# Seven half products instead of eight for the u and r weights of the first block

## The reference, cut to what matters

```
h_lat, h_ctx = modulate(rmsnorm(x)), modulate(rmsnorm(ctx))     # 1024 and 256 tokens
u, v, q, k, vv, r, af, ab, ga, gb = split(h @ w_in)             # u, v, vv, r, ga, gb: 1024 columns each
lf, lb = log_sigmoid(af @ w_af + b_af) / 16, ...                # the decays
o = scan over chunks of 64 tokens with q, k, vv, lf, lb         # both directions
b_lat = norm(o) * silu(r);  a_lat = gelu(u) * mixed(layernorm(gelu(v)))
y = sigmoid(ga) * (a_lat @ w_a) + sigmoid(gb) * (b_lat @ w_b)
```

## Time and profile before

| | |
|---|---|
| median of 3 runs | 3249.92 us (3249.72 to 3252.65) |
| the profiled execution's own time | 3249.49 us |
| its span, first to last instruction | 3248.2 us |
| PE busy | 3175.4 us, 98% of the span |
| DVE, ACT, POOL busy | 1892.3, 1408.1, 393.3 us |
| granted PE clock | 0.993 of full |

### The profile page before, as it was taken

The page is one execution under the profiler, slowest core; times in us unless marked ns, Lnnn a source line. Parts: engine busy times, 40 slices in busy tenths (PEclk is TensorE's granted clock), DMA queues, the critical chain, the costliest instruction groups (busy, mean ns, idle before and its releaser), DMA issues.

```text
span 3248.2 us, 38749 instructions
## 1 busy us (share of the span) xinstructions
PE 3175.4 (98%) x14558; PEld 2584.2 (80%) x14558; DVE 1892.3 (58%) x3053; ACT 1408.1 (43%) x2336; POOL 393.3 (12%) x625
## 2 busy tenths in 40 slices
PE   6999999999999999999999999999899999999998
PEld 4888788888888878888888887877667888888886
DVE  5562344565334487777444546656686787776443
ACT  4791232254333243333233376575576443333221
POOL 1111000012000200000010200112221200001011
PEclk8999999999999999999999999999999999999999
DMA  5564544456542323334763444355876432336652
GB/s 231 180 223 157 166 149 155 127 209 217 177 143 101 132 98 111 112 115 144 242 197 95 144 136 137 124 172 170 178 114 154 149 123 104 123 104 216 207 189 68
DMA packets 228489, 495.13 MB, mean 152 GB/s; under 512 B 21712, under 2 KB 84816, under 8 KB 226768
## 3 DMA queue, kind: packets, MB, share of 16 engines
q1 hardware_dynamic: 146688, 298.11, 29.2%
q0 software_dynamic: 81616, 194.55, 19.0%
HBM read 353.63 MB, written 138.94 MB: 152 GB/s over the span
## 4 chain that ended last, share of the span: by engine, by line
PE 85%; DVE 7%; ACT 3%; DMA 2%; issue 2%; POOL 0%; SPq 0%; DVEq 0%; POOLq 0%; ACTq 0%
PE p L2273 12%; PE p L2275 12%; PE p L2274 12%; PE p L319 12%; PE p L321 11%; PE p L320 11%; PE p L420 2%; PE p L421 2%; PE p L422 2%; PE p L3341 1%; PE p L1287 1%; PE p L3327 1%; PE p L1276 1%; DMA s_qs<-d_q2l 1%; DMA s_ad<-i_ada 1%
## 5 line engine op out<-in xcount | busy, mean ns | idle before, releaser
L319 PE MATMUL p<-s_xh,s_wh 128*128 128x512 f32 x1936 | 767.1, 396 | 9.8 <-DVE s_tmp L476 6.0
L321 PE MATMUL p<-s_xh,s_wl 128*128 128x512 f32 x1936 | 754.9, 390 | 0.0
L320 PE MATMUL p<-s_xl,s_wh 128*128 128x512 f32 x1936 | 754.3, 390 | 0.0
L2273 PE MATMUL p<-s_xh,s_wh 128*128 128x512 f32 x1152 | 449.7, 390 | 1.5 <-DVE s_wl L2522 1.3
L2275 PE MATMUL p<-s_xh,s_wl 128*128 128x512 f32 x1152 | 448.3, 389 | 0.0
L2274 PE MATMUL p<-s_xl,s_wh 128*128 128x512 f32 x1152 | 448.2, 389 | 0.0
L319 PEld LDWEIGHTS p<-s_xh,s_wh 128*128 128x128 f32 x1936 | 363.6, 188 | 96.6 <-issue 11.1
L321 PEld LDWEIGHTS p<-s_xh,s_wl 128*128 128x128 f32 x1936 | 363.5, 188 | 76.8
L320 PEld LDWEIGHTS p<-s_xl,s_wh 128*128 128x128 f32 x1936 | 363.8, 188 | 74.3 <-issue 1.9
L278 DVE TENSOR_TENSOR s_wl<-s_ws,s_wh 128x1024 fp32r<-128x1024 f32 x143 | 176.7, 1247 | 208.6 <-ACT s_wh L271 208.3
L464 ACT ACTIVATE s_tmp<-p 128x512 f32<-128x512 f32 (+1 forms) x157 | 93.0, 593 | 429.3 <-PE p L321 340.8
(11 more groups left out here) (437 smaller groups left out, 5497.4 us busy)
## 6 DMA issues: line engine op xcount, KB each, us to landing
d_h<-s_fhl POOLq DMA_DIRECT2D x80, 512.0 KB, 3.0
s_ws<-i_Wf SPq DMA_DIRECT2D x48, 512.0 KB, 4.2
s_qb<-i_Wf SPq DMA_DIRECT2D x40, 512.0 KB, 4.2
s_qb<-i_Wf SPq DMA_DIRECT2D x80, 256.0 KB, 2.9
s_ws<-i_Wf SPq DMA_DIRECT2D x80, 256.0 KB, 2.8
s_aw<-i_adaT SPq DMA_DIRECT2D x32, 512.0 KB, 3.7
s_xh<-d_h POOLq DMA_DIRECT2D x16, 1024.0 KB, 12.3
s_xl<-d_h POOLq DMA_DIRECT2D x16, 1024.0 KB, 15.4
```

What stands on the lines that cost most here:

```text
L319: pe.matmul(o, wh, H[:, k, c:c + n], start=(k == 0), stop=False)
L320: pe.matmul(o, wh, L[:, k, c:c + n], start=False, stop=False)
L321: last = pe.matmul(o, wl, H[:, k, c:c + n], start=False, stop=(k == 7))
L2273: pe.matmul(o, wh[:, c], H[:, k, :], start=(start and k == 0), stop=False)
```

## The change

The order of weights becomes ga 0 to 2, v, ga 3 to 7, gb; u and r leave the list of fill jobs.

- **Pairs.** u and r are made at the end of stage 1, as 8 pairs of two weight tiles (256 output rows). A pair is a product of two by two blocks: four blocks of weights (128 outputs by 512 inputs) with four of tokens (512 inputs by 512 tokens). It is made from seven units, each 4 k tiles by 3 matmuls, 12 matmuls of 512 columns. Partial results are passed from bank to bank by ACT (`seeded`), P5 is held in SBUF (`held`) and added by DVE when P7 and P3 are taken out. Two matmuls mark banks 5 and 6 as written before the first pair.
- **Sums.** DVE makes the four combined token blocks once (40 operations of 128x512, 16 low parts, ACT 16 high parts), beside stage 1's jobs 21 to 26, and for each pair four combined weight blocks (`fold_dve`). High and low parts of units are made by halves of a tile, seven units ahead.
- **Pieces.** In the last job of the second vv group and of both v groups, the four weight tiles of the group are taken one after the other, so that each frees its place early: 96 matmuls of 128 columns in place of 24 of 512.
- **Places.** Raw tiles of v and vv use `ACC` and `RB` too, and only the first vv group uses the second set of places.
- **Moved.** Stage 1 has 31 fill jobs, with the decay units two at a time behind chosen jobs (Abs twice, Exp twice, Ln twice) and 8 of the dots; the other 24 dots run beside the pairs, three in each, behind P5, P2 and P4. Stage 2 has 22 fill jobs: ga 0 to 2 (6) and both v groups (16), three in slot 0 and one in each slot after it. Stage 3 has 26, and the norms, mixes and outputs of its second half move one job up and on.

The diff, cut to its core:

```diff
-    for n in ("v", "u", "r", "ga", "gb"):
-        order += [(n, m) for m in range(8)]
+    order += [("ga", m) for m in range(3)] + [("v", m) for m in range(8)]
+    order += [("ga", m) for m in range(3, 8)] + [("gb", m) for m in range(8)]
...
+SEVEN = ("P1", "P5", "P6", "P2", "P7", "P3", "P4")
+SEVEN_TILES = [(n, m) for n in ("u", "r") for m in range(0, 8, 2)]
+SEVEN_FIRST = 17
...
+        x = 2 + m % 2 if name in ("v", "vv") and m % 4 > 1 else i if i < NW else i % NS
...
+            p.pieces = []
+            if chunk == chunks[-1][0]:
+                p.pieces = pieces
+                for a in pieces[:-1]:
+                    used[i - 3 + a] = mm.at(more("mm"))
...
+        for a in p.pieces:
+            for k in range(8):
+                xh, xl = H[:, k, p.col:p.col + 128], L[:, k, p.col:p.col + 128]
+                wh, wl = WHg[:, a, k * 128:k * 128 + 128], WLg[:, a, k * 128:k * 128 + 128]
+                pe.matmul(o[:, a, :], xh, wh, start=(k == 0), stop=False)
+                pe.matmul(o[:, a, :], xl, wh, start=False, stop=False)
+                last = pe.matmul(o[:, a, :], xh, wl, start=False, stop=(k == 7))
+            last.then_inc(*mm.up())
+        if p.pieces:
+            return
...
-            plan_rows(jobs, "vv", group, banks, dV, "v", of_context + token_chunks(2, (0, 1)))
-        plan_rows(jobs, "v", 0, banks, dVm, "vm", token_chunks(0, (0, 1)))
+        plan_rows(jobs, "vv", 0, banks, dV, "v", of_context + token_chunks(2, (0, 1)))
+        second_places_done = jobs[-1].mm
+        plan_rows(jobs, "vv", 1, banks, dV, "v", of_context + token_chunks(2, (0, 1)), (1, 2, 3, 0))
+        context_done = jobs[22].mm
...
+        decay_after = (0, 1, 3, 4, 6, 8, 9, 11, 12, 14, 16, 17, 19)
+        dot_after = (2, 5, 7, 10, 13, 15, 18, 20)
+        steps = []
+        for j in range(31):
+            steps += [("before", j), ("fill", j)]
+            if j in dot_after:
+                steps.append(("dot", dot_after.index(j)))
+            if j in decay_after:
+                steps.append(("decay", decay_after.index(j)))
...
+        def difference_dve(o, one, other):
+            (h1, l1), (h2, l2) = one, other
+            dv.tensor_tensor(o, h1, h2, ALU.subtract).then_inc(*summed.up())
+            DVW.wait_ge(*summed.now())
+            dv.tensor_tensor(o, o, l1, ALU.add).then_inc(*summed.up())
+            DVW.wait_ge(*summed.now())
+            dv.tensor_tensor(o, o, l2, ALU.subtract).then_inc(*summed.up())
...
+            dv.tensor_tensor(THL[t][1][:, k, :], TF[t][:, k, :], THL[t][0][:, k, :].bitcast(F), ALU.subtract).then_inc(*t_lo.up())
...
+        B11, B21, B22 = ((XH[:, k:k + 4, c:c + 512], XL[:, k:k + 4, c:c + 512]) for k, c in ((0, 0), (4, 0), (4, 512)))
+        INPUT = {"P1": B11, "P2": B21, "P3": B22, "P5": THL[1], "P6": THL[2], "P7": THL[3], "P4": THL[4]}
+        BANK = {"P1": BA, "P5": BF, "P6": BB, "P2": BA, "P7": BE, "P3": BB, "P4": BE}
...
+                u.slot = (2 + u.i) % 8
+                u.hi, u.lo, u.mm = u_hi.at(u.i + 1), u_lo.at(u.i + 1), mm.at(more("mm"))
+                u.slot_free = units[u.i - 8].mm if u.i >= 8 else used[13 + u.slot // 2]
...
+        dots_of_pair = [range(8 + 24 * n // n_pairs, 8 + 24 * (n + 1) // n_pairs) for n in range(n_pairs)]
...
+            for i in range(2):
+                sp.dma_start(x[:, 1024 * i:1024 * i + 1024], D["W" + p.name][p.m + i]).then_inc(*raw[2 * (p.n % 2) + i].up())
...
+            for p in pairs:
+                if p.n + 2 < n_pairs:
+                    load_pair_sp(pairs[p.n + 2])
+                elif p.n + 2 == n_pairs:
+                    weights_sp(SEVEN_FIRST + NS)
+                for j in dots_of_pair[p.n]:
+                    if j + 1 < 32:
+                        dot_sp(j + 1)
+            weights_sp(SEVEN_FIRST + NW + NS)
...
+        def unit_pe(u, fresh):
+            wh, wl = half_tile(u.slot)
+            o = B[u.bank][:, :]
+            PEW.wait_ge(*u.hi)
+            PEW.wait_ge(*u.lo)
+            H, L = u.x
+            for k in range(4):
+                c = slice(128 * k, 128 * k + 128)
+                for t in u.x_ready[k]:
+                    PEW.wait_ge(*t)
+                pe.matmul(o, wh[:, c], H[:, k, :], start=(fresh and k == 0), stop=False, skip_group_check=not fresh)
+                pe.matmul(o, wh[:, c], L[:, k, :], start=False, stop=False, skip_group_check=not fresh)
+                x = pe.matmul(o, wl[:, c], H[:, k, :], start=False, stop=(k == 3), skip_group_check=not fresh)
+            x.then_inc(*mm.up())
...
+            for b in (BB, BE):
+                for t in first_free[b]:
+                    PEW.wait_ge(*t)
+                pe.matmul(B[b][:, :], XH[:, 0, 0:128], XH[:, 0, 0:512], start=True, stop=True)
+            for p in pairs:
+                for name in SEVEN:
+                    if name == "P1":
+                        for t in ([pairs[p.n - 1].outs["P2"].ev] if p.n else first_free[BA]):
+                            PEW.wait_ge(*t)
+                    elif name == "P5":
+                        for t in ([pairs[p.n - 1].held] if p.n else first_free[BF]):
+                            PEW.wait_ge(*t)
+                    elif name in ("P6", "P2"):
+                        PEW.wait_ge(*p.seed1)
+                    elif name in ("P7", "P3"):
+                        PEW.wait_ge(*p.seed2)
+                    elif name == "P4":
+                        PEW.wait_ge(*p.outs["P7"].ev)
+                    unit_pe(p.units[name], name in ("P1", "P5"))
...
+            ac.activation(half_tile(u.slot)[0], u.src, ACT.Copy).then_inc(*u_hi.up())
...
+        def pair_act(p, name):
+            u = p.units[name]
+            if name == "P1":
+                ACW.wait_ge(*u.mm)
+                for t in ([pairs[p.n - 1].outs["P3"].ev] if p.n else first_free[BB]):
+                    ACW.wait_ge(*t)
+                ac.activation(B[BB][:, :], B[BA][:, :], ACT.Copy).then_inc(*seeded.up())
+            elif name == "P5":
+                ACW.wait_ge(*u.mm)
+                if p.n:
+                    ACW.wait_ge(*pairs[p.n - 1].outs["P3"].ev)
+                ac.activation(HELD[:, :], B[BF][:, :], ACT.Copy).then_inc(*held.up())
+            elif name == "P6":
+                ACW.wait_ge(*u.mm)
+                for t in ([pairs[p.n - 1].outs["P4"].ev] if p.n else first_free[BE]):
+                    ACW.wait_ge(*t)
+                ac.activation(B[BE][:, :], B[BB][:, :], ACT.Copy).then_inc(*seeded.up())
+            elif name in ("P2", "P4"):
+                out_act(p.outs[name], u.bank, u.mm)
...
+            high_act(6)
+            for u in units:
+                pair_act(pairs[u.n], u.name)
+                high_act(u.i + 7)
+                tail_weights(weights_act, u)
...
+            if units[i].name == "P5":
+                DVW.wait_ge(*p.raw0)
+                DVW.wait_ge(*p.raw1)
+                DVW.wait_ge(*(pairs[p.n - 1].units["P3"].lo if p.n else w_lo.at(SEVEN_FIRST)))
+                dv.tensor_tensor(S1, p.A21, p.A22, ALU.add).then_inc(*folded.up())
+                DVW.wait_ge(*p.s[0])
+                dv.tensor_tensor(S2, S1, p.A11, ALU.subtract).then_inc(*folded.up())
+            elif units[i].name == "P7":
+                if p.n:
+                    DVW.wait_ge(*pairs[p.n - 1].units["P7"].lo)
+                dv.tensor_tensor(S3, p.A11, p.A21, ALU.subtract).then_inc(*folded.up())
+            else:
+                DVW.wait_ge(*p.s[1])
+                dv.tensor_tensor(S4, p.A12, S2, ALU.subtract).then_inc(*folded.up())
...
+                dv.tensor_tensor(l, u.src, h.bitcast(F), ALU.subtract).then_inc(*u_lo.up())
...
+            dv.tensor_tensor(TMP[:, o.slot, :], B[u.bank][:, :], HELD[:, :], ALU.add).then_inc(*evD.up())
...
+            for i in range(7):
+                low_dve(i)
+            for u in units:
+                p = pairs[u.n]
+                pair_dve(p, u.name)
+                fold_dve(u.i + 8)
+                low_dve(u.i + 7)
+                for j, after in zip(dots_of_pair[p.n], ("P5", "P2", "P4")):
+                    if u.name == after:
+                        mod_dve(j)
+                tail_weights(weights_dve, u)
+            mods_end_dve()
...
-        items = [("u", m, False, "plain", dU, "u", 1.0, TC) for m in range(8)] + [("r", m, False, "plain", dR, "r", 1.0, TC) for m in range(8)]
+        items = [("ga", m, False, "plain", dGA, "ga", 1.0, TC) for m in range(3)]
         banks = [0, 1]
-        jobs = []
-        plan_rows(jobs, "v", 1, banks, dVm, "vm", token_chunks(0, (0, 1)))
-        for j in range(4):
-            jobs[2 * j].make = 26 + j
-        rows_done = jobs[7].mm
-        jobs += plan_fill(items, banks, None, parts, [])
+        jobs = plan_fill(items, banks, None, parts, [])
+        plan_rows(jobs, "v", 0, banks, dVm, "vm", token_chunks(0, (0, 1)), (0, 1, 2, 3))
+        plan_rows(jobs, "v", 1, banks, dVm, "vm", token_chunks(0, (0, 1)), (0, 1, 2, 3))
+        for p in jobs:
```

(92 more changed lines are left out.)

277 lines of the change are left out of this document (211 added, 66 removed).

## The result

The changed kernel takes 3264.17 us (3262.23 to 3269.65, 5 runs), the kernel before 3249.92 (3248.23 to 3252.65, 5 runs): ratio 1.0047, interval 1.0036 to 1.0058. It is slower by 14 us. The forecast was 3240.0 us (3225 to 3256), so it missed by 24.2 us and in sign. The profiled execution took 3262.23 us.

What follows compares the result with a forecast made beforehand. PE, busy 98% of the span, was taken as the bound. Terms -21.8 + 0.5 + 15.3 - 5.2 + 1.0 + 0.2 + 0.3 = -9.7 us took 3249.5 to 3239.8, stated as 3240 us, range 3225 to 3256.

Steps and rivals of the forecast that it cites:

- What lies beside other work: Stage 1 and pairs: ACT's and DVE's work stays covered by PE's; only +0.3 us, for eight pairs of products.
- the signs of being wrong that the prediction names: The pieces' step is off, or PE gains long waits in the pairs or in stage 2's slots.
- Products, -21.8: u and r, end of stage 1: 672 matmuls of 512 columns instead of 768, 96 fewer at 0.2276 us, -21.8 us.
- the rival of the dots: Pairs of products: dots bound them if adaT landings slow to 5.5 us (3252) or 6 us (3264); 13%.
- Pieces, +15.3: Three row jobs: 96 matmuls of 128 columns for 24 of 512, 0.110 us each, +5.1 us a job, +15.3 us.
- both rivals of its size: Pieces: weight loads hide (0.057 us, 3224.5 to 3231.5, 12%), or float32 pace (0.248 us, 3279.5, 10%).
- Start of stage 2, -5.2: Stage 2's start: 5.5 us lost to idle time and fallen clock; three jobs cover it, 0.3 us stays: -5.2 us.
- Slots of stage 2 and stage 3: Stage 2: one job covers each slot, about 12.8 us in the later half, +1.0 us; stage 3: jobs moved, +0.2 us.
- the +1.0 of the forecast: Stage 2's slots: the state product's wait for ACT's key copy, 0.7 us each time, grows by 1.05.

Runs made afterwards that it cites:

- e1: Kernel before with only stage 1's decay units two at a time, at the changed kernel's places among the jobs: 3265.87 us, ratio 1.0053.
- e2: Changed kernel with the second half of each decay pair (subtraction and scans) right behind its first half in VectorE's order: 3252.39 us, ratio 1.0012.
- e8: Changed kernel with the edit of e2, and stage 1's eight dots moved behind job 20: 3245.12 us, ratio 0.9992.
- e10: Changed kernel with the decay units using four banks in turn instead of two: 3262.13 us, ratio 1.0045.
- e5: Changed kernel with its 24 decay units one at a time, spread over the same 20 jobs, dots unmoved: 3256.15 us, ratio 1.0023.
- e4: Changed kernel with the three row jobs of stages 1 and 2 whole again, without pieces: 3257.19 us, ratio 1.0027.
- e6: Kernel of e2 with stage 2's first job ahead of the first slot's gate step in every engine's order: 3247.89 us, ratio 1.0001.
- e7: Kernel of e6 with the three row jobs whole again, without pieces: 3240.47 us, ratio 0.9971.

## Why the prediction was wrong

**The step that failed** stands under "What lies beside other work": "ACT in stage 1 loads its tables half as often; before, it was 64% busy there and PE never waited." It costed the decay pairs at nothing from a busy share and a count of loads. The share was an average over 227 us; from 95 to 225 us, where the decay units run, ScalarE was busy 88% (113.91 of 130). The table loads did fall, from 42 to 22 in that stretch, and ScalarE's busy time to 84.36 us. But a share of busy time says nothing of a loop with only two buffers: one unit at a time left the other buffer for the next Abs; two at a time leave none. In short, what ScalarE saved in loads it lost in waiting for scans (34.9 us). And the loop, 10.6 us a pair, had only 8.8 us of PE's work to hide behind, since the units also moved closer together. No rival held this mechanism, and the signs of being wrong that the prediction names, waits in the pairs of products or in the slots, look elsewhere. Shown by e1 (+17 us by the pairs at this spacing, with no new products), e2 and e8 (back by the order of scans and dots, pairs and spacing kept), e10 (not PE's banks). The missing term is +18.7 us. What grouping and spacing each cost alone was not run in the kernel before.
The Trainium skill (ScalarE: Activation LUTs, Rules for kernel authors) advises to do all of one table set before switching. Here doing so about halved the loads, and e1, which does it, is 17 us slower. With the scans no longer behind other work, the pairs (e2, 3252.39) ran 3.8 us under single units in the same jobs (e5, 3256.15).

**Products, -21.8**: right. The pairs run from 300.3 to 452.68 us, 152.4 us, where 153 were expected, without a wait. Outputs of P7 cost nothing that shows, and the rival of the dots falls: the 23 rows of `adaT` from 300 to 455 us landed in a median of 3.7 us, as before.

**Pieces, +15.3**: the step of 0.111 us was taken as 0.110, so both rivals of its size are out. The 0.110 was the middle between two rows and not derived, so its fit is partly luck. The Trainium skill (TensorE: Matmul & The Clock Gate, Back-to-back issue gap) gives about 81 ns for a sustained pair at 128 columns; these float32r matmuls took 0.111 us. Three jobs cost 15.6 us of PE. What the term left out is the other side, the stalls that whole jobs would have: net, the pieces cost 7.0 us (e4) and 7.4 (e6 to e7). The change is better without them; as a term beside the kernel before, +15.3 stands.

**Start of stage 2, -5.2**: right in kind, too large. "The third job needs job 0's bank, which ACT copies behind its first exponentials, at about the same time" saw the queue and priced it at 0.3 us. From 452.68 to the first transposes are 18.8 us, against some 16.7 foreseen: +2.1, with PE idle 2.17 and the granted clock at 1.00. In e2 the same wait was 3.33, and moving one line of the order brought 4.5 us.

**Slots of stage 2 and stage 3**: right. A slot takes 679.43 - 666.64 = 12.79 us, as foreseen, and PE is idle in none of the later ones. The slowest key copy makes PE wait 1.68 us instead of 0.74, and the four waits for it sum to 3.9 us against 2.9: the +1.0 of the forecast. In stage 3 PE is idle 0.9 us, as before.

**The account.** Stage 1 +18.7 and stage 2's start +2.1 make 20.8 of the miss of 24.2. At 1.1 ms both kernels run the same code; a line of it in the kernel after, then in the one before:
```profile
1114.65 0.95 PE L2003 MATMUL p<-s_ones,s_acc 128*128 128x1 f32 x8
```
```profile
1103.08 0.94 PE L1648 MATMUL p<-s_ones,s_acc 128*128 128x1 f32 x8
```
+11.6 there, where -9.7 was forecast: a miss of 21.3. Of the last 3 us, 1.1 arise behind this place, in code that didn't change (2146.2 us to the end of the span against 2145.1); PE's waits at L332 for VectorE are 7.4 us against 6.0 there. The other 1.9 are no part of this trace: the profiled execution of the changed kernel took 3262.23 us, 1.9 under the median. No run tells more, and both are within what executions of one kernel differ by.

## What to carry to other kernels

Before grouping units to save a fixed cost on one engine, write down the loop through the buffers they share: what must end before the next group may begin, on every engine, with what is queued ahead of it. If the group takes all buffers, the engines take turns, and the loop's length has to be less than the work it hides behind; busy shares don't show it, least of all averaged over a stage in which the group's work fills only a part. When a wait appears, look two engines back: four banks moved the wait from one line to another and shortened stage 1 by 0.6 us; an order of VectorE shortened it by 11.9. And where a job frees several places at once, whatever refills them arrives as one burst ahead of the next small urgent copy.
